# A hybrid encoder layer on one core: the column piece read with each open quad becomes 1024 wide

## The reference, cut to what matters

```python
h = h + y @ w_out
out = 0
for e in range(32):
    hdn = silu(t @ w1[e]) * (t @ w3[e])          # t = rmsnorm(h), w1, w3: 2048 x 512
    out = out + combine[:, e:e+1] * (hdn @ w2[e])  # w2: 512 x 2048
h = h + out
pe = rmsnorm(p @ w_ple)
gate = sigmoid(rmsnorm(h) @ w_pg + b_pg)         # w_pg: 2048 x 2048
h = h + gate * pe
```

## Time and profile before

| what | value |
|---|---|
| time, median of 3 runs | 1354.26 us (1350.98 to 1354.38) |
| span of the profiled execution | 1348.8 us |
| PE busy | 1071.9 us, 79% of the span |
| DVE, ACT, POOL busy | 26%, 12%, 5% |
| bytes read from HBM | 473.12 MB, 352 GB/s over the span |
| chain that ended last | DMA 49%, PE 46%, SP queue 3% |
| first matmul of `out_unit` to the end of the span | 1314.98 to 1348.8 us |

### The profile page before, as it was taken

How to read it: one execution, slowest core, us unless ns; L and a number is a source line. 1 busy time by engine, 2 the same in 40 slices (tenths; PEclk the granted TensorE clock), 3 DMA queues, 4 the chain that set the end, 5 groups by cost and what they waited for, 6 DMA issues and landing times.

```text
span 1348.8 us, 13912 instructions
## 1 busy us (share of the span) xinstructions
PE 1071.9 (79%) x5992; PEld 499.0 (37%) x5992; DVE 357.4 (26%) x516; ACT 160.1 (12%) x319; POOL 65.8 (5%) x66
## 2 busy tenths in 40 slices
PE   8999999999975876766576665767576656899998
PEld 4468887446432322222222222323232212333333
DVE  1843736963421121221112120000000000111116
ACT  1112316003210110000000000000000000000002
POOL 0112112300000020000000000000000000000000
PEclk9999999999998888888888888877778888999999
DMA  9637333366999999999999999999999999999991
GB/s 352 230 116 259 125 125 125 125 248 257 411 412 428 430 431 429 427 427 429 428 429 431 430 421 429 415 427 427 415 429 415 426 427 411 389 392 389 395 350 62
DMA packets 89470, 476.15 MB, mean 353 GB/s; under 512 B 10096, under 2 KB 10496, under 8 KB 67904
## 3 DMA queue, kind: packets, MB, share of 16 engines
q1 hardware_dynamic: 83312, 471.88, 86.0%
q0 software_dynamic: 560, 2.88, 0.6%
q10 hardware_dynamic: 5536, 0.47, 0.3%
HBM read 473.12 MB, written 2.10 MB: 352 GB/s over the span
## 4 chain that ended last, share of the span: by engine, by line
DMA 49%; PE 46%; SPq 3%; issue 1%; DVE 0%; ACT 0%; DVEq 0%
DMA ring<-in_w 49%; PE ps L1638 8%; PE ps L1920 6%; PE ps L1759 5%; PE ps L2000 4%; PE ps L1605 4%; PE ps L2095 3%; PE ps L1582 2%; PE ps L1798 2%; PE ps L2055 2%; PE ps L2113 2%; PE ps L1886 2%; SPq L543 1%; SPq L534 1%; PE ps L1879 1%; PE ps L2068 1%
## 5 line engine op out<-in xcount | busy, mean ns | idle before, releaser
L2000 PE MATMUL ps<-ring,area 128*32 128x512 f32 x1024 | 164.5, 796 | 122.1 <-DMA ring<-in_w 122.1
L1920 PE MATMUL ps<-ring,area 128*32 128x512 f32 x976 | 149.2, 731 | 109.1 <-DMA ring<-in_w 109.1
L1358 DVE TENSOR_TENSOR h<-ps,h 128x2048 f32<-128x2048 f32 x32 | 73.3, 2291 | 288.5 <-PE ps L1886 288.4
L2000 PEld LDWEIGHTS ps<-ring,area 128*32 128x32 f32 x1024 | 43.3, 138 | 228.8 <-issue 228.8
L1638 PE MATMUL ps<-hT,ring 128*128 128x256 f32 x512 | 112.9, 380 | 0.0
L1920 PEld LDWEIGHTS ps<-ring,area 128*32 128x32 f32 x976 | 31.9, 123 | 206.3 <-issue 205.9
L1638 PEld LDWEIGHTS ps<-hT,ring 128*128 128x128 f32 x512 | 96.5, 190 | 14.0 <-issue 1.2
L1413 DVE TENSOR_TENSOR hT<-area,ps 128x128 f32<-128x128 f32 x16 | 4.6, 287 | 314.9 <-ACT area L946 314.9
L1879 PE MATMUL ps<-area,hs 128*128 128x128 f32 x512 | 64.3, 279 | 0.6 <-DVE area L1339 0.6
L1964 PE MATMUL ps<-ring,area 128*32 128x512 f32 x496 | 58.0, 608 | 8.3 <-DMA ring<-in_w 8.3
L1879 PEld LDWEIGHTS ps<-area,hs 128*128 128x128 f32 x512 | 59.6, 192 | 10.3 <-issue 10.3
(11 more groups left out here) (327 smaller groups left out, 1021.6 us busy)
## 6 DMA issues: line engine op xcount, KB each, us to landing
ring<-in_w SPq DMA_DIRECT2D x126, 2048.0 KB, 20.7
ring<-in_w SPq DMA_DIRECT2D x63, 1024.0 KB, 14.9
ring<-in_w SPq DMA_DIRECT2D x14, 4096.0 KB, 25.2
ring<-in_w_in SPq DMA_DIRECT2D x28, 1024.0 KB, 14.2
ring<-in_w_out SPq DMA_DIRECT2D x16, 1024.0 KB, 8.3
ring<-in_w_pg SPq DMA_DIRECT2D x11, 1024.0 KB, 14.5
area<-in_w SPq DMA_DIRECT2D x2, 2048.0 KB, 14.4
hs<-in_w SPq DMA_DIRECT2D x4, 1024.0 KB, 14.5
```

The costliest lines, as they stand in the source:

```text
L1358: dve.tensor_tensor(h[:, t, :], ps[:, bank:bank + 4, :].rearrange("p b n -> p (b n)"), h[:, t, :], ALU.add).then_inc(acc_done, 1)
L1920: ins = mm(ps[SLOTS * g:SLOTS * g + SLOTS, 0, :], XG[:, b, k, SLOTS * e:SLOTS * e + SLOTS], s[:, D_EXP * kk:D_EXP * kk + D_EXP], start=(k ...
L2000: ins = mm(ps[SLOTS * g:SLOTS * g + SLOTS, 0, :], XG[:, b, k, SLOTS * e:SLOTS * e + SLOTS], s[:, D_EXP * kk:D_EXP * kk + D_EXP], start=(k ...
```

## The change

- The piece read with each open quad is 1024 columns wide (`WIDE`). Its four loads are of 2 MB, with rows of 4 KB, each issued as one DMA into two chunks.
- `w2_open` does both 512-column halves, `copy_open_y` copies two results, and `scatter_open` scatters two. These sums no longer gather in PSUM over the quads: `add_open` adds each quad's result to `h` at once.
- The last stage has only pieces 2 and 3, so eight steps instead of twelve. A step is `w2_piece`, then three gate units with the scatter after the first. Pieces 0 and 1 are both turned in the first step.
- The loads are reordered to match, with w2 before w_pg.

The diff, cut to its core:

```diff
+FIRST = 2
+WIDE = 512 * FIRST
+QUAD_PAIRS = 2 * W13_CHUNKS + 4
+OPEN_ADDS = 2 * OPEN_QUADS
+UNITS_A_STEP = 3
...
+def column_steps():
+    return [(i, q) for i in range(FIRST, PIECES) for q in range(OPEN_QUADS)]
...
 def piece_loads():
     order = []
-    for i in range(1, PIECES):
-        w2_ = [("w2", i, q, k) for q in range(OPEN_QUADS) for k in range(4)]
-        w_pg_ = [("w_pg", i - 1, kk, 0) for kk in range(4)]
-        order += w_pg_ + w2_
+    for s, (i, q) in enumerate(column_steps()):
+        order += [("w2", i, q, k) for k in range(4)]
+        for v in range(UNITS_A_STEP * s, UNITS_A_STEP * s + UNITS_A_STEP):
+            if v % 8 == 0:
+                order += [("w_pg", v // 8, kk, 0) for kk in range(4)]
     return order + [("w_pg", PIECES - 1, kk, 0) for kk in range(4)]
...
-                    for half in range(2):
-                        sp_q.dma_start(ring[:, slot + half, :].rearrange("p (e n) -> p e n", e=QUAD),
-                                       w2_v[e:e + QUAD, :, 2 * (r - 16) + half, 0:512].rearrange("e p n -> p e n")
-                                       ).then_inc(open_loaded[slot + half], 16)
+                    sp_q.dma_start(ring2(slot).rearrange("p (e n) -> p e n", e=QUAD),
+                                   w2_v[e:e + QUAD, :, r - 16, 0:WIDE].rearrange("e p n -> p e n")
+                                   ).then_inc(open_loaded[slot], 16)
...
+            def copy_open_y(q):
+                act.wait_ge(open_used, QUAD_CHUNKS * (q + 1))
+                if q:
+                    act.wait_ge(piece_ps, NT * q)
+                for half in range(2):
+                    act.activation(Ys[:, half, :], ps[:, 4 + half, :], ACT.Copy).then_inc(y_copied, 1)
...
+            def add_open(q):
+                for t in range(NT):
+                    dve.wait_ge(piece_ps, NT * q + t + 1)
+                    piece = h[:, t, 0:WIDE]
+                    dve.tensor_tensor(piece, ps[:, 4 + 2 * t:6 + 2 * t, :].rearrange("p b n -> p (b n)"), piece, ALU.add
+                                      ).then_inc(h_final, 1)
...
+            def w2_open(q):
+                pe_.wait_ge(open_hdn, QUAD * (q + 1))
+                if q:
+                    pe_.wait_ge(h_final, NT * q)
+                for k in range(4):
+                    slot = open_loaded_pair(QUAD_PAIRS * q + 16 + k)
+                    rows = ring[:, slot:slot + 2, :].rearrange("p s n -> p (s n)")
+                    for half in range(2):
+                        for e in range(QUAD):
+                            at = WIDE * e + 512 * half
+                            ins = mm(ps[SLOTS * e:SLOTS * e + SLOTS, 4 + half, :], HDNs[:, QUAD * q + e, k, :],
+                                     rows[:, at:at + 512], start=(k == 0), stop=(k == 3))
+                    ins.then_inc(open_used, 2)
+
+            def scatter_open(q):
+                pe_.wait_ge(y_copied, 2 * (q + 1))
+                pe_.wait_ge(open_g, q + 1)
+                for t in range(NT):
+                    for half in range(2):
+                        ins = mm(ps[:, 4 + 2 * t + half, :], Gs[:, q, t, :], Ys[:, half, :], start=True, stop=True)
+                    ins.then_inc(piece_ps, 1)
...
-            scatter_piece(0, OPEN_QUADS - 1)
-            turn_piece(0)
-            for i in range(1, PIECES):
-                for q in range(OPEN_QUADS):
-                    gate_unit(i - 1, 2 * q)
-                    if q < OPEN_QUADS - 1:
-                        gate_unit(i - 1, 2 * q + 1)
-                    w2_piece(i, q)
-                    if q:
-                        scatter_piece(i, q - 1)
-                scatter_piece(i, OPEN_QUADS - 1)
-                gate_unit(i - 1, 7)
-                turn_piece(i)
+            scatter_open(OPEN_QUADS - 1)
+            for s, (i, q) in enumerate(column_steps()):
+                w2_piece(i, q)
+                if s == 0:
+                    turn_piece(0)
+                    scatter_piece(i, q)
+                    turn_piece(1)
+                elif q == 0:
+                    turn_piece(i - 1)
+                for n in range(UNITS_A_STEP * s, UNITS_A_STEP * s + UNITS_A_STEP):
+                    gate_unit(n // 8, n % 8)
+                    if s and n == UNITS_A_STEP * s:
+                        scatter_piece(i, q)
+            turn_piece(PIECES - 1)
```

More of the change, by code:

```diff
@@ L125, in open_pair_used, with piece_uses @@
     return QUAD_CHUNKS * q + in_quad
+def column_steps():
+    return [(i, q) for i in range(FIRST, PIECES) for q in range(OPEN_QUADS)]
+def piece_uses():
+    order = []
+    for s, (i, q) in enumerate(column_steps()):
+        order += [("w2", i, q, k) for k in range(4)]
+        for v in range(UNITS_A_STEP * s, UNITS_A_STEP * s + UNITS_A_STEP):
+            if v % 8 == 7:
+                order += [("w_pg", v // 8, kk, 0) for kk in range(4)]
+    return {load: OPEN_CHUNKS + n + 1 for n, load in enumerate(order)}
+PIECE_USES = piece_uses()
 def w2_used(i, q, k):
[L130 to L132 removed]
+    return PIECE_USES["w2", i, q, k]
 def w_pg_used(i, kk):
[L137 removed]
+    return PIECE_USES["w_pg", i, kk, 0]
 def out_units():
@@ L166, in place_pieces @@
         free[slot] = (open_pair_used(g), g // PAIRS + 1)
-        free[slot + 1] = (open_pair_used(g), OPEN_QUADS if g % QUAD_PAIRS >= 16 else 0)
+        free[slot + 1] = (open_pair_used(g), 0)
     gathered = QUAD_CHUNKS * (OPEN_QUADS - 2) + 4 * W13_CHUNKS
@@ L177, in place_pieces @@
         placed[load] = (place, after, uses + 1)
-        free[place] = (w2_used(i, q, k) if what == "w2" else w_pg_used(i, q), uses + 1)
+        free[place] = (PIECE_USES.get(load, math.inf), uses + 1)
     return placed
@@ L933, in copy_y, with copy_turned, square_piece @@
                 act.wait_ge(open_used, w2_used(i, q, 3))
-                if m >= 2:
-                    act.wait_ge(piece_ps, m - 1)
+                act.wait_ge(piece_ps, max(m - 1, OPEN_ADDS))
                 act.activation(Ys[:, m % 2, :], ps[:, 4 + m % 2, :], ACT.Copy).then_inc(y_copied, 1)
+            def copy_open_y(q):
[4 more added lines that the diff above has]
+                    act.activation(Ys[:, half, :], ps[:, 4 + half, :], ACT.Copy).then_inc(y_copied, 1)
+            def copy_turned(i):
+                act.wait_ge(turn_ps, 2 * i + 1)
+                for kk in range(2):
+                    act.activation(hT_pieces[:, i % 2, kk, :], ps[:, 2, T * kk:T * kk + T], ACT.Copy,
+                                   scale=gain(1, 4 * i + kk)).then_inc(turn_act, 1)
+            def square_piece(i):
+                for t in range(NT):
+                    act.wait_ge(ss_ready, 1 + NT * i + t)
+                    act.activation(junk_piece, h[:, t, 512 * i:512 * i + 512], ACT.Square,
+                                   accum_out=pieces[:, 0, t, i:i + 1]).then_inc(ss_ready, 1)
             for j in range(OPEN):
@@ L948, in _ @@
                 if j % QUAD == QUAD - 1:
-                    copy_y(0, j // QUAD)
-            for i in range(PIECES):
-                if i:
-                    for q in range(OPEN_QUADS):
[L954 to L962, removed]
+                    copy_open_y(j // QUAD)
+            for i, q in column_steps():
+                copy_y(i, q)
+                if q == 0:
+                    copy_turned(i - 1 if i > FIRST else 0)
+                    if i == FIRST:
+                        copy_turned(1)
+                        square_piece(0)
+                    square_piece(i - 1)
+            copy_turned(PIECES - 1)
+            square_piece(PIECES - 1)
             for u, (t, at, width, _) in enumerate(OUT_UNITS):
@@ L1511, in add_gate @@
                     dve.tensor_tensor(piece, ps[:, u % 2, :], piece, ALU.add).then_inc(gate_added, 1)
+            add_open(OPEN_QUADS - 1)
             dve.wait_ge(rp_ready, 1)
[L1514 to L1521, removed]
+            copy_turned(0)
+            copy_turned(1)
+            for s, (i, q) in enumerate(column_steps()):
+                if i > FIRST and q == 0:
+                    copy_turned(i - 1)
+                for n in range(UNITS_A_STEP * s, UNITS_A_STEP * s + UNITS_A_STEP):
+                    add_gate(n // 8, n % 8)
+                    if q == OPEN_QUADS - 1 and n == UNITS_A_STEP * s:
+                        add_piece(i)
+            copy_turned(PIECES - 1)
             dve.wait_ge(ss_ready, 1 + 2 * PIECES)
```

34 lines of the change are left out of this document (14 added, 20 removed).

## The result

The changed kernel takes 1364.88 us (median of 4 runs, 1363.98 to 1365.98) against 1354.32 us for the kernel before, a ratio of 1.0092 with a 95% interval from 1.0077 to 1.0106: **10.6 us slower**. A second comparison on another occasion gave 1.0084 (1.0067 to 1.0102). The profiled execution took 1365.03 us with a span of 1363.3 us. Its span is 14.5 us longer than that of before, more than the medians differ. The times of the runs stand some 1.7 us and more above their spans, so the profiled execution of before, with 1348.8 us, was probably its quickest, the one of 1350.98 us.

What follows compares the result with a forecast made beforehand. DMA alone was taken to bind the quads, DMA and PE both the last stage, with PE binding it after the change. Quads +38.5 and stage -25.4 give +13.1 us on 1354.26, so 1367.4; range 1359 to 1374.

Steps and rivals of the forecast that it cites:

- Quads, +38.5 us: Four open quads: each swaps four 1 MB loads for four of 2 MB, growing 9.6 us, 38.5 in all.
- T: The moment the fourth open quad's last load lands, from which the prediction followed the last stage.
- The cover in the quads, costed at nothing: Open quads: added PE, ACT and DVE work hides behind the loads, costing nothing; without that cover 5.5 us a quad.
- The stage bound by PE, T + 146.1: Last stage: PE binds, out units begin 146.1 us after the fourth quad's last landing, making the stage 25.4 us shorter.
- the seams: Last stage: 1.6% of 122 us, 2.0 us, added for time the summed PE work had missed in the stage before.
- the start: Last stage's beginning: first gate unit done 22.1 us after the quads' last landing, two more units by 29.1.
- the check of the stage before: Old last stage: summed PE work and waits gave 160.1 us where the trace has 162.6, 1.6% short.
- That the loads end the stage: Rival, last stage: loads still end it, 38.2 us shorter, 1354.5 or 1350.8 in all; chance 0.09.
- That the wider row gains nothing: Rival, quads: wider rows cost what 2 KB rows do, +18.0 us, 1372; chance 0.08.
- A slow start: Rival, last stage's beginning: PE's lower clock slows three gate units, +10 us, 1377; chance 0.08.

Runs made afterwards that it cites:

- the late load: Load of b_pg moved behind nearly all last-stage loads: in the changed kernel 1.0053 against the kernel before; in the kernel before itself 0.9976.
- the doubled matmuls: Changed kernel with 32 more w2 matmuls in each open quad, done into a free bank: 1.0089 against the kernel before.
- the old order: Changed kernel with the first four w_pg loads and first three gate units put ahead of the stage's first w2 piece: 1.0109 against the kernel before.
- the cut loads: Changed kernel with each wide load of the quads cut into two of 512 columns, rows of 2 KB: 1.0111 against the kernel before.

## Why the prediction was right

The forecast was +13.1 us and 1367; measured are +10.6 and 1364.88, inside the range. In the traces both parts moved as forecast, the quads by 2 us more and the stage by 3.8 us more, and these two errors partly cancel. Step by step:

- **Quads, +38.5 us.** Measured +40.5 from the first column load to the last landing. The price itself was right: the spacing grew by 9.5 us a quad against 9.6 in the sum, and the 4 KB row costs 2.58 us where 2.56 was interpolated. The missing 2 us come in the fourth quad, from a load that the prediction didn't look at. POOL issues b_pg (1 MB) when all but four chunks of the open quads are used. Before, that was at 1136.90, 6.5 us ahead of the landing T, and it landed 3.1 us behind T. In the changed kernel four chunks are two wide loads, and it is issued at 1176.75, 10.4 us ahead, so that all of it lies ahead of T. The run with the late load took 3.6 us back. With the late load in both kernels the quads grow by 37.1 us, so without b_pg the forecast of 38.5 is 1.4 too high.
- **The cover in the quads, costed at nothing:** right, shown by the doubled matmuls.
- **The stage bound by PE, T + 146.1:** the mechanism is right; the length was 142.3. A step takes 15.8 us (1231.83 to 1247.62) against 15.9. What was too much are the seams (2.0), about 0.7 in the start, and 1 us in the steps, where a w2 piece takes 3.57 rather than 3.67 and a scatter 1.72 rather than 1.82. The seams were a misreading. The 2.5 us by which the check of the stage before fell short are for the most part its first two gate units, which took 8.42 us (1152.35 to 1160.77) instead of 6.96 since they began at a lower clock (0.65 in the line below). In the changed kernel the clock was full again before the first gate unit, so this was not to be added.

```profile
1152.30:1156.40 4.10, 4.05 (x7) 1.81 (x8) 0.00 (x0) 0.81 (x3) 0.00 (x0) 0.65 1.04 386
```

- **The start:** the end of the first three units was forecast at T + 29.1 and came at T + 28.5. But its reason was half wrong. I had PE wait about 3 us for w_pg; it waited 0.35, since at the lower clock (0.58 granted from 1187 to 1197.5) the last w2 matmuls took 3.64 us instead of 1.92 and the scatter 5.53 instead of 3.70. The two ways of losing the same time don't add, which is why the old order gained nothing, and why my expectation of that run failed.
- **Rivals.** That the loads end the stage: excluded, DMA is idle for its last 14 us and more, and 43 us of loads less gave it 3. It would have been so with 10 to 13 us of matmuls less; the prediction had said 13. That the wider row gains nothing: the trace of the cut loads speaks against it. The Trainium skill (DMA: Bandwidth & Descriptors, Specifications) has the line rate reached from 512 B on. The traces don't agree, but between 2 KB and 4 KB the gain is only 0.13 us in 2.71. A slow start: it exists, with some 3.5 us lost at the lower clock, but lies in the shadow of the loads: in the run with the late b_pg it is gone, and the stage is 142.5 us nevertheless.

The gain that one might expect of taking 43 us of loads out of the stage went two ways. 14 us of it were never there: PE could follow only by the 27 us that its own path became shorter, and by 2 us of waits for loads. And the 40 us that came back in the quads stand in full, since nothing there overlaps with DMA but work that was hidden already.

## What to carry to other kernels

Where two engines are both full in one stage, taking work from the one gains only what the other is relieved of, and the work moved is paid in full where it goes if that place is bound by the same engine. Compare the two engines' sums for the stage before a byte is moved; halve the work of each in turn on the chip, as here, to see how far the second bound is away. And look for small transfers on other queues that share the engines: moving one of 1 MB behind nearly all loads of the last stage made the kernel before 0.24% faster, while the change made it 0.9% slower.

## What the runs showed that I had not expected

One DMA of 1 MB from another queue doesn't wait for its turn: in the changed kernel two loads ahead of T were 7.6 us apart instead of 5.1, while b_pg itself landed 8.4 us after its issue. It took its share from the loads of the SP queue: the quad's last one was issued at 1160.26, 16.5 us before b_pg, and landed 2.0 us after it. And the stage had the same length whether its first 10 us ran at the lower clock, with 0.35 us of waits for loads in it (142.3 us), or at the full clock with 3.5 us of such waits (142.5 us).
